# A gated-linear-attention mixer: both directions of a level in one product, two heads at a time

## The reference, cut to what matters

```
z = x @ w_in;  q, k, v, r, glr = split(z)          # 4 heads, q and k 128 wide, v 256 wide
loga = log_sigmoid(glr @ gate_w + gate_b) / 16     # one decay per token, head, channel and direction
# in each direction, b = cumsum(loga):
A[t, s] = sum_d q[t, d] * exp(b[t, d] - b[s, d]) * k[s, d]     # s <= t (s >= t backwards)
o = A_fwd @ v + A_bwd @ v
out = (silu(r) * head_norm(o)) @ w_out
```

## Time and profile before

| | |
|---|---|
| median of 3 runs | 1702.24 us (1699.68 to 1702.92) |
| the profiled execution | 1700.06 us |
| its span, first to last instruction | 1698.3 us |
| mean granted PE clock | 0.929 of full speed |
| PE busy | 1360.0 us (80%) |
| DVE, ACT, POOL busy | 312.4, 223.1, 68.8 us |
| HBM read | 498.83 MB, 294 GB/s over the span |
| the GLA mixer in the trace | about 629 to 804 us |
| the second mixture of experts | about 804 to 1280 us |

### The profile page before, as it was taken

How to read it: one execution, slowest core, us unless ns; L and a number is a source line. 1 busy time by engine, 2 the same in 40 slices (tenths; PEclk the granted TensorE clock), 3 DMA queues, 4 the chain that set the end, 5 groups by cost and what they waited for, 6 DMA issues and landing times.

```text
span 1698.3 us, 19946 instructions
## 1 busy us (share of the span) xinstructions
PE 1360.0 (80%) x8535; PEld 766.1 (45%) x8535; DVE 312.4 (18%) x733; ACT 223.1 (13%) x426; POOL 68.8 (4%) x88
## 2 busy tenths in 40 slices
PE   8998867658667679998777667667568999999996
PEld 6453424224223236564434223224225854788843
DVE  1163200000000121454310000000003032222201
ACT  1131001001000011340100001001001032121100
POOL 1011000000000000350100000000000000000000
PEclk9998998889889779999899898889879999999999
DMA  9824699999999998222699999999999530344100
GB/s 329 328 75 187 277 429 427 430 428 428 430 427 429 428 406 306 99 100 86 250 430 426 430 428 428 429 428 430 428 417 381 167 123 23 126 151 152 70 0 25
DMA packets 84895, 500.58 MB, mean 295 GB/s; under 512 B 6108, under 2 KB 31056, under 8 KB 60272
## 3 DMA queue, kind: packets, MB, share of 16 engines
q1 hardware_dynamic: 81664, 489.05, 70.9%
q0 software_dynamic: 3184, 10.87, 1.8%
HBM read 498.83 MB, written 1.07 MB: 294 GB/s over the span
## 4 chain that ended last, share of the span: by engine, by line
PE 53%; DMA 39%; DVE 5%; ACT 1%; issue 1%; POOL 0%; SPq 0%; DVEq 0%; ACTq 0%
DMA weight_ring<-in_moe_w_down 21%; DMA weight_ring<-in_moe_w_up 17%; PE bank L1005 9%; PE bank L631 7%; PE bank L889 5%; PE bank L670 5%; PE bank L1037 4%; PE bank L648 4%; PE bank L929 3%; PE bank L919 3%; PE bank L636 2%; PE bank L870 2%; PE bank L818 1%; PE bank L941 1%; PE bank L602 1%
## 5 line engine op out<-in xcount | busy, mean ns | idle before, releaser
L889 PE MATMUL bank<-weight_ring,phase_room 128*32 128x256 f32 x4096 | 267.0, 412 | 129.8 <-DMA weight_ring<-in_moe_w_up 108.6
L889 PEld LDWEIGHTS bank<-weight_ring,phase_room 128*32 128x32 f32 x4096 | 134.9, 116 | 259.2 <-DMA weight_ring<-in_moe_w_up 89.4
L919 PE MATMUL bank<-weight_ring,phase_room 128*32 128x512 f32 x1024 | 163.8, 773 | 109.3 <-DMA weight_ring<-in_moe_w_down 104.2
L1005 PE MATMUL bank<-xT,weight_ring 128*128 128x256 f32 (+1 forms) x768 | 153.2, 362 | 1.6 <-DVE xT L1309 0.9
L929 PE MATMUL bank<-phase_room 128*128 128x512 f32 x256 | 128.5, 648 | 31.8 <-DVE phase_room L1637 31.8
L1005 PEld LDWEIGHTS bank<-xT,weight_ring 128*128 128x128 f32 x768 | 136.0, 190 | 18.6 <-ACT xT L1066 2.1
L919 PEld LDWEIGHTS bank<-weight_ring,phase_room 128*32 128x32 f32 x1024 | 33.2, 126 | 206.5 <-DMA weight_ring<-in_moe_w_down 112.4
L631 PE MATMUL bank<-xT,weight_ring 128*128 128x256 f32 x512 | 113.2, 383 | 1.8 <-DMA weight_ring<-in_mlstm_w_in 1.1
L929 PEld LDWEIGHTS bank<-phase_room 128*128 128x128 f32 x256 | 50.3, 207 | 125.3 <-issue 125.3
L631 PEld LDWEIGHTS bank<-xT,weight_ring 128*128 128x128 f32 x512 | 98.0, 192 | 17.7 <-issue 2.7
L1632 DVE TENSOR_TENSOR phase_room<-phase_room,bank 128x256 f32<-128x256 f32 x32 | 13.5, 421 | 460.5 <-PE bank L889 460.5
(11 more groups left out here) (227 smaller groups left out, 925.6 us busy)
## 6 DMA issues: line engine op xcount, KB each, us to landing
weight_ring<-in_moe_w_gate SPq DMA_DIRECT2D x64, 2048.0 KB, 35.6
weight_ring<-in_moe_w_up SPq DMA_DIRECT2D x64, 2048.0 KB, 33.9
weight_ring<-in_moe_w_down SPq DMA_DIRECT2D x64, 2048.0 KB, 35.7
weight_ring<-in_w_up SPq DMA_DIRECT2D x22, 1024.0 KB, 7.6
weight_ring<-in_gla_w_in SPq DMA_DIRECT2D x6, 2048.0 KB, 21.8
weight_ring<-in_w_qkv SPq DMA_DIRECT2D x6, 2048.0 KB, 23.3
weight_ring<-in_mlstm_w_in SPq DMA_DIRECT2D x5, 2048.0 KB, 16.9
weight_ring<-in_w_down SPq DMA_DIRECT2D x5, 2048.0 KB, 7.8
```

Source lines behind the costliest of these rows:

```text
L889: last = mm(bank[q * CAP:(q + 1) * CAP, 0:S], xinT[:, 4 * r + k, j * CAP:(j + 1) * CAP], w[:, k, q * S:(q + 1) * S], start=(r == 0 and k = ...
L919: last = mm(PS[i][k * CAP:(k + 1) * CAP, :], hidT[:, 4 * r + k, :], w[:, k, i * 512:(i + 1) * 512], start=(r == 0), stop=(r == 1), skip_gr ...
L1005: last = mm(PS[bank_pair + c // 2][:, at + tokens.start:at + tokens.stop], w[:, k, c * P:(c + 1) * P], xT[:, k, tokens], start=(k == 0), s ...
```

## The change

A step now is one level of two heads (x = 0 or 1) in both directions, again 16 steps. The queries of a step are written for all 128 tokens of a tile: the right halves with the forward factor, the left halves with the backward factor; the keys the other way round. One product of 128 by 128 per head and tile then holds both directions, and one mask per level picks the pairs of neighbouring blocks. POOL makes the differences of two heads and both directions in one instruction, in access patterns with one dimension more, of which one steps backwards; queries and keys are separate steps (32 in all), with four buffers where there were two. Each exponential and each scaling has its own semaphore count.

PE's order changes: piece 2 starts when the first projection's banks have been read, piece 3 joins pieces 4 to 7 in the levels (40 calls, 5 to a level, 2 ahead of the first half and 3 ahead of the second). ACT's takes of these pieces move accordingly. DVE does its running sums ahead of its half of the key projection. POOL multiplies the first gate part by the gain after the levels rather than in them. The gate columns product is packed: contraction chunk k goes to rows 32 (k % 4) of the bank, the sum over the four groups is made by the following product, whose weights `gate_w_sb` are loaded four times (8 small transfers for 2).

```diff
+        masks[:, lv] = (i[:, None] // L) == (i[None, :] // L ^ 1)
...
-    q_dec = mix_t[:, 2048:3072].rearrange("p (d n) -> p d n", d=2)
+    q_diff_t = mix_t[:, 2048:3072]
...
-    k_dec = acc_t[:, :].rearrange("p (d n) -> p d n", d=2)
-    diffs = gate[:, :, 512:1024]
+    def moved(ap, offset, *dims):
+        return bass.AP(ap.tensor, ap.offset + offset, [ap.ap[0], *dims])
+    qk_dec = acc_t[:, :].rearrange("p (w n) -> p w n", w=2)
+    diffs = [[q_diff_t[:, 512 * x:512 * (x + 1)] for x in range(2)], [gate[:, x, 512:1024] for x in range(2)]]
...
+    glrT = room[:, 8992:9248]
...
-        for d in range(2):
-            pool.dma_start(gate_w_sb[RANK * d:RANK * (d + 1), d], t["gla_gate_w"][0, d]).then_inc(small_landed[3], 16)
+        for q in range(4):
+            for d in range(2):
+                r = 2 * RANK * q + RANK * d
+                pool.dma_start(gate_w_sb[r:r + RANK, d], t["gla_gate_w"][0, d]).then_inc(small_landed[3], 16)
...
-        for i in range(2 * (len(LEVELS) + 1)):
-            d, L = i % 2, P >> (i // 2)
...
+        HS = H * S
+        for i in range(4 * N_LEVELS):
+            L, x, key = P >> (i // 4), (i // 2) % 2, i % 2
+            blocks = [[2 * L, 512 // (2 * L)]]
+            border = moved(b_t, 512 * x + L - 1, [HS + 1, 2], *blocks, [0, L])
+            to = diffs[key][x]
+            if i >= 4:
+                pool.wait_ge(decays_exp, i - 3)
+            if key:
+                last = nc.gpsimd.tensor_tensor(moved(to, 0, [L, 2], *blocks, [1, L]), border,
+                                               moved(b_t, 512 * x, [HS + L, 2], *blocks, [1, L]), ALU.subtract)
+            else:
+                last = nc.gpsimd.tensor_tensor(moved(to, L, [-L, 2], *blocks, [1, L]),
+                                               moved(b_t, 512 * x + L, [HS - L, 2], *blocks, [1, L]), border,
+                                               ALU.subtract)
+            last.then_inc(diffs_done, 1)
+        output_gate(1, 0)
...
             for k in range(KC):
-                last = mm(PS[4][0:2 * RANK, 0:S], wglr[:, k, :], xT[:, k, :], start=(k == 0), stop=(k == KC - 1))
+                q = k % 4
+                last = mm(PS[4][32 * q:32 * q + 32, 0:S], wglr[:, k, :], xT[:, k, :],
+                          start=(k < 4), stop=(k >= 4), skip_group_check=True)
             last.then_inc(glr_done, 1)
...
-            pe.wait_ge(small_landed[3], 48)
+            pe.wait_ge(small_landed[3], 16 * 9)
...
             project(T_GLA + 2, 1, 1, (0, 1))
+            pe.wait_ge(proj_act, taken(1, 0))
+            pe.wait_ge(proj_dve, taken(1, 0))
+            piece(1, T_GLA + 3, 2, PS[0])
             pe.wait_ge(proj_act, taken(1, 1))
             pe.wait_ge(proj_dve, taken(1, 1))
-            for n in (2, 3):
-                piece(1, T_GLA + 3, n, PS[n % 2])
...
-            pe.wait_ge(piece_out, pieces_before(1) + 4)
             pe.wait_ge(diag_placed, 1)
-            for i in range(2 * (len(LEVELS) + 1)):
-                d = i % 2
-                if d == 0:
-                    n, half = 4 + i // 4, (i // 2) % 2
-                    if n >= 6 and half == 0:
+            pe.wait_ge(z_ready, 1)
+            def fill(first, last):
+                while first < last:
+                    n, k = 3 + first // KC, first % KC
+                    stop = min(KC, k + last - first)
+                    if k == 0 and n >= 5:
                         pe.wait_ge(piece_out, pieces_before(1) + n - 1)
-                    piece(1, T_GLA + 4 + (n - 4) // 2, n, PS[2 + n % 2], range(4 * half, 4 * half + 4))
-                pe.wait_ge(scaled_done, i + 1)
-                if i >= 2:
-                    pe.wait_ge(placed, i - 1)
...
+                    piece(1, T_GLA + 3 + (n - 2) // 2, n, PS[2 + n % 2], range(k, stop))
+                    first += stop - k
+            for m in range(2 * N_LEVELS):
+                lv, x = divmod(m, 2)
+                fill(5 * lv + 2 * x, 5 * lv + 2 + 3 * x)
+                if m == 0:
+                    pe.wait_ge(piece_out, pieces_before(1) + 3)
+                pe.wait_ge(scaled_done, 2 * m + 2)
+                if m >= 2:
+                    pe.wait_ge(placed, m - 1)
+                for c in range(2):
+                    for h in (2 * x, 2 * x + 1):
+                        tq = 1 - c if lv == 0 else c
+                        at = (2 * c + h % 2) * P
+                        last = mm(PS[x][:, at:at + P], qk_dec[:, 1, h * S + c * P:h * S + (c + 1) * P],
+                                  qk_dec[:, 0, h * S + tq * P:h * S + (tq + 1) * P], start=True, stop=True)
                 last.then_inc(prod_done, 1)
-            pe.wait_ge(placed, 2 * (len(LEVELS) + 1))
+            pe.wait_ge(placed, 2 * N_LEVELS)
...
-            for n in (2, 3):
-                take_values(n, PS[n % 2])
-            for i in range(2 * (len(LEVELS) + 1)):
-                d = i % 2
+            for i in range(4 * N_LEVELS):
+                x, key = (i // 2) % 2, i % 2
                 act.wait_ge(diffs_done, i + 1)
-                if i >= 2:
-                    act.wait_ge(scaled_done, i - 1)
-                for w in range(2):
-                    last = f(PS[4 + 2 * d + w][:, :], diffs[:, w], ACT.Exp, scale=1.0 / GLA_TAU)
-                last.then_inc(decays_exp, 1)
-                if i in (3, 7):
-                    n = i // 4
+                if i >= 4:
+                    act.wait_ge(scaled_done, i - 3)
+                f(PS[4 + 2 * x + key][:, :], diffs[key][x], ACT.Exp, scale=1.0 / GLA_TAU).then_inc(decays_exp, 1)
+                if i == 1:
+                    take_values(2, PS[0])
+                elif i == 4 * 2 + 3:
+                    take_values(3, PS[3])
+                elif i in (4 * 4 + 3, 4 * 5 + 3):
+                    n = i // 4 - 4
                     take_gate(pieces_before(1) + 4, n, PS[2 + n % 2], ACT.Silu)
-            act.wait_ge(decays_exp, 2 * (len(LEVELS) + 1))
...
-            take_projection(1, T_GLA + 2, 1)
...
+            take_projection(1, T_GLA + 2, 1)
...
-            def scale(i):
-                d, L = i % 2, P >> (i // 2)
-                dve.wait_ge(decays_exp, i + 1)
-                if i >= 2:
-                    dve.wait_ge(prod_done, i - 1)
...
+            def scale(m):
+                x = m % 2
+                if m >= 2:
+                    dve.wait_ge(prod_done, m - 1)
+                for w in range(2):
+                    dve.wait_ge(decays_exp, 2 * m + w + 1)
+                    c = w * H * S + 512 * x
+                    v.tensor_tensor(qk_dec[:, w, 512 * x:512 * (x + 1)], qkT_t[:, c:c + 512],
+                                    PS[4 + 2 * x + w][:, :], ALU.mult).then_inc(scaled_done, 1)
+            def place(m):
+                lv, x = divmod(m, 2)
+                dve.wait_ge(prod_done, m + 1)
+                if m >= 2:
+                    dve.wait_ge(placed, m - 1)
+                src = PS[x][:, :].rearrange("p (c h n) -> p c h n", c=TT, h=2)
+                if lv == 0:
+                    last = v.tensor_copy(moved(gb_t[:, :], 2 * x * S + P, [H * S - P, TT], [S, 2], [1, P]), src)
                 else:
...
+                    mask = level_masks[:, (lv - 1) * P:lv * P]
+                    last = v.copy_predicated(moved(gb_t[:, :], 2 * x * S, [H * S + P, TT], [S, 2], [1, P]),
+                                             moved(mask, 0, [0, TT], [0, 2], [1, P]), src)
                 last.then_inc(placed, 1)
...
```

More of the change, by code:

```diff
@@ L82, in constants @@
     main = np.concatenate([ident, flip, after, before, slots, logit_of], 1)
-    n = np.arange(64)
-    masks = np.zeros((P, 2, len(LEVELS), 64), np.float32)
+    masks = np.zeros((P, len(LEVELS), P), np.float32)
     for lv, L in enumerate(LEVELS):
[L86 to L89, removed]
+        masks[:, lv] = (i[:, None] // L) == (i[None, :] // L ^ 1)
     dist = np.arange(S)[::-1]
@@ L346, in link @@
             self.eng.wait_ge(self.s, self.n)
+    N_LEVELS = len(LEVELS) + 1
+    def moved(ap, offset, *dims):
+        return bass.AP(ap.tensor, ap.offset + offset, [ap.ap[0], *dims])
     U_X0, U_Y0, U_M0, U_X1, U_Y1, U_M1, U_ATT, U_FFN, U_OUT = range(9)
@@ L796, in gla @@
                 last.then_inc(diag_done, 1)
-            pe.wait_ge(piece_out, pieces_before(1) + 4)
             pe.wait_ge(diag_placed, 1)
-            for i in range(2 * (len(LEVELS) + 1)):
-                d = i % 2
-                if d == 0:
-                    n, half = 4 + i // 4, (i // 2) % 2
-                    if n >= 6 and half == 0:
-                        pe.wait_ge(piece_out, pieces_before(1) + n - 1)
-                    piece(1, T_GLA + 4 + (n - 4) // 2, n, PS[2 + n % 2], range(4 * half, 4 * half + 4))
-                pe.wait_ge(scaled_done, i + 1)
-                if i >= 2:
-                    pe.wait_ge(placed, i - 1)
-                for h in range(H):
-                    if i < 2:
```

(36 more changed lines are left out.)

26 lines of the change are left out of this document (2 added, 24 removed).

## The result

The changed kernel's median is 1683.89 us (1682.16 to 1685.26, 4 runs); the kernel before stands at 1702.58 us (1699.68 to 1708.87, 4 runs). The ratio is 0.9878, with a 95% interval of 0.9855 to 0.9900: 1.2% less, and the medians differ by 18.7 us, where the prediction had 16.1 us, 0.95%. The time lies inside the range, 0.4 us from its lower end. As a ratio it does not: 1683.5 us is 0.9890 of the 1702.24 us from which the prediction started, and 0.9878 is lower. The forecast's ratio, 0.9905, is just outside the interval. Direction and mechanism are right, the size of the gain is too small. The profiled execution took 1682.6 us against 1700.06 us, its span is 1680.8 us.

The account below looks back on a forecast made before the run. PE was taken to bound the GLA mixer's levels, with time won there passed on through the transfer-bound experts. 13.6 us from the stretch plus 2.5 us from packing made 16.1 us: 1702.2 to 1686.1 us, range 1683.5 to 1697 us.

Parts of the forecast that it names:

- the range: Whole kernel: 1683.5 us (nothing lost at the changes, POOL's earlier start fully used) to 1697 us (slower POOL instructions).
- PE bounds the levels; buffers alone win little: GLA mixer's levels: PE busy 55.71 of 59.00 us, the POOL, ACT and DVE ring only just faster; fewer PE instructions win.
- The product's price: Level products on PE: 64 calls at 0.2525 us, taken from the diagonal's 8 calls in 2.02 us, 16.2 us together.
- the stretch: End of key projection to start of value products: 63.1 us forecast against 76.76 us before, 13.6 us won.
- The other terms of the stretch: Piece 2 6.99, diagonal 2.02 and 0.83, pieces 35.0, closings 0.9, changes 0.4, last placing 0.8 us.
- The packed product: Gate columns product on the chain of waits: 1.07 us instead of 3.61 us, 2.5 us won.
- Passed on one for one: Second mixture of experts: time won before its ninth tile, issued at 829.91 us, moves the whole rest earlier.
- The base: Profiled execution of the kernel before, 1700.06 us, on which the sum was made; 2.2 us below the 1702.24 us median.
- Exclusion of POOL and DVE: Rival in the levels: full exclusion gives 1703 us, or 1710 us with slower POOL; chances 0.04 no change, 0.04 slower.
- a slow POOL: Rival in the levels: POOL instructions between 1.6 and 2.0 us lose up to 13 us, 1690 to 1699 us; chance 0.06.
- Stops at the handovers: Rival in the levels: PE waits in each level for a scaling, 0.7 us a level, giving 1692 us; chance 0.13.
- The gain not passed on: Rival behind the mixer: the experts' stream starts no earlier or loses its lead, giving 1701 us; chance 0.03.

Follow-up runs that it names:

- narrow run: Changed kernel with 64 of the 128 query columns in each level product; median 1681.29 us, ratio 0.9880 to the kernel before.
- packed variant: Kernel before with the packed gate columns alone; median 1702.18 us, ratio 0.9993 to the kernel before.
- 376 more: Changed kernel with an unneeded POOL subtraction of 376 elements behind each difference; median 1693.70 us, ratio 0.9938 to the kernel before.
- serial buffers: Changed kernel with POOL beginning a difference only after the previous one's exponential; median 1692.54 us, ratio 0.9942 to the kernel before.

## Why the prediction was right or wrong

- *PE bounds the levels; buffers alone win little.* Right, shown from both sides: twice the products cost 14.3 us, more buffers in the kernel before win 2.0 us. In the changed kernel a POOL that waits for each exponential costs 7.2 us, so there the added buffers have a part, though how much a single pair would cost isn't shown. Not quite right is that the chain before stood on PE almost all the time: from 701.0 to 715.3 us it stood on the other engines. The prediction's own count of the stops there, 2.3 us, is close to the 2.0 us that the buffers won back.
- *The product's price.* This is the step that failed: "8 calls in 2.02 us, 0.2525 us a call". The 2.02 us are the busy time of a group that ends in a wait, so they hold the whole length of one product and not only its share of the stream, 0.2 us more, which in a stream lies under the neighbouring instructions. The spacing of the same 16 records in the chain of waits is 1.80 us in the changed kernel. At 0.2225 us, 64 calls are 14.2 instead of 16.2 us. In the chain they took 14.5, since the last group ends in a wait (15 of 0.89 and one of 1.14 us): 1.7 of the 2.5 us by which the stretch is shorter than forecast. I had the right number at hand in the 3.52 us for 16 calls, and read a difference between the two as the price of columns; the narrow run shows that there is none.
- *The other terms of the stretch* give the remaining 0.8 us. A piece call in the stream costs 0.86 us instead of 0.875, but behind the diagonal's stop and where a tile is closed three groups took 0.25 us more (1.98 for 1.72 us), so 40 calls took 35.2 us for 35.0. The closings took 0.7 for 0.9 us, the changes between pieces and products nothing instead of 0.4, the diagonal with its stop 2.6 instead of 2.85, piece 2 6.87 for 6.99, the last placing 0.80 for 0.83.
- *The packed product.* Right: 1.07 us for 3.61. With the stretch's 16.2 us the chain gives 18.7 us; 16.1 was the sum.
- *Passed on one for one.* Right in the sum: ninth tile 17.9 us earlier, 868.8 us behind it. That the sum comes out so well is partly luck, since beside the 18.7 us the clock moved single rows both ways: the mixer's first piece took 7.13 us after 9.14 in the trace before, the first output projection 9.14 us after 7.13, the transposes ahead of it 0.8 us more. The loss behind the levels is no single case: from the value products to the ninth tile the kernel before takes 67.0 or 67.1 us in three of its four traces, and the changed kernel with its variants 68.2 to 71.1 us in nine of ten.
- *The range.* Its low end, 1683.5 us, left nothing for a product cheaper than the row, though the price of the product was the one term with two rows to choose from, 0.22 and 0.2525 us. With it the low end would have been 1681.6 us.
- *The base.* The sum was made on one execution, 2.2 us below the median of three, and that was itself below the 1704 us of the later 49 runs. The changed kernel's profiled 1682.6 us is near its usual 1683.5. It could explain why the medians of the later rounds differ by 21 us and the two spans by 17.5; that isn't shown. That the changed kernel has fewer drops on average isn't shown: in the stretch there were none in ten traces of its family, and some in two of five of the kernel before and its packed variant. In the first output projection it is the other way round: nine of the ten took 8.6 to 10.2 us, two of the five 8.83, the others 7.13 (and the kernel before with more buffers 8.83 too). So the change may lose there a part of what it wins.
- *The rivals.* Exclusion of POOL and DVE and a slow POOL both fall (1.04 and 1.10 us an instruction, overlapped throughout). By the rule of the Trainium skill, SBUF — State Buffer, section "SBUF: two separate sides", the scalings with one input in PSUM leave POOL alone; the traces agree, with POOL's 1.04 and 1.10 us in both kernels. Stops at the handovers: none in the levels beyond the 0.7 us of the three closings. The gain not passed on: falls.

## What to carry to other kernels

Take the price of an instruction in a stream from the spacing in the chain of waits, not from the busy time of a group that ends in a wait; for short fp32 products the two differed by 12%, over 64 calls 2 us. Where weight loads set the pace, fill the width: a product of 128 columns cost what one of 64 did, so two directions in one product and a mask behind it halve the cost. What buffers are worth depends on how fast the bounding engine is: 2 us before the products were halved, while full serialization of POOL and ACT cost 7 us after.

## What the runs showed of the hardware

PE's granted clock drops from the higher of its two levels, 2.4 GHz, to the lower, 1.2 GHz, for short times also in the middle of the levels: in the longest trace of the kernel before it is 0.50 of full speed from 748 to 754 us. One piece of 8 records then takes 5.18 or 5.48 us instead of 3.49, the first piece of the mixer 8.8 to 9.2 us instead of 7.13. The places differ from execution to execution of the same kernel: the first output projection took 7.13 us in three of the four traces of the kernel before and 8.83 us in the fourth, and 9.14 us in the changed kernel's, whose table of stretches shows the clock at 0.74 there:

```profile
752.00:763.00 11.00, 10.31 (x24) 4.82 (x23) 4.08 (x12) 1.38 (x3) 0.00 (x0) 0.74 0.15 58
```

Ahead of it PE had waited for the head norm. The two drops in the levels also came within some 2 us of a stop of 0.9 us, for a scaling. But the same stop stands in the other traces of the kernel before without a drop, and the changed kernel with a slowed POOL has stops of 2.1 and 3.2 us in its levels (376 more, serial buffers) at a clock of 1.00. So a stop alone doesn't bring a drop, and what does is open. Each drop costs 1.3 to 3.1 us. In the longest trace of the kernel before (1709.09 us) the rows from the key projection to the ninth expert tile hold 7 of the 9 us more (3.3 in the stretch, 3.8 behind it). For changes of a few microseconds, a stretch between two marks in one trace at full clock tells more than a dozen timed runs.
